# Page-number reads and block sums moved between two stages of a hybrid decoder step, and ScalarE's order in the Mamba layer changed

## What is computed

```python
# SSD mixer, cut
proj = h @ w_in; z, xbc, dt = split(proj)
conv = silu(causal_conv(xbc)); xs, bm, cm = split(conv)
y = sum over s<=t of exp(cum_t - cum_s) * (cm_t . bm_s) * dt_s * x_s   # prompt
new_state = state * exp(dt*a) + (dt*x) outer bm                        # each decode sequence
y = (y + d_skip * xs) * silu(z)
y = y * rsqrt(mean over 512 of y*y + 1e-5) * norm_g ; out = y @ w_out
# end of a layer: two layer norms, experts between them
h = h + sigmoid(h @ ple_gate) * (p @ ple_proj)
# NSA, decode: keys and values of the cache, squeezed to one per 64 rows
past_cmp = kv_pool[page_table, :, 0:2]
kvc = einsum('bnlckd,clk->bnckd', blocks, softmax(pos_w))
```

## Time and profile before

| what | value |
| --- | --- |
| median of 3 runs | 1118.59 us (1118.05 to 1122.78) |
| profiled execution, its own time | 1118.43 us |
| its span in the trace | 1116.7 us |
| outside the span | 1.7 us |
| PE, DVE, ACT, POOL busy | 93%, 44%, 27%, 15% |
| stages, start in the trace | SSD 0, tail 0 about 291 us, NSA 596.4 us, tail 1 about 815 us |

### The profile page before, as it was taken

One profiled execution on the slowest core, in us unless ns is written; L12 is line 12 of the kernel. 1 busy time (PEld: TensorE's weight loads), 2 busy tenths in 40 slices (PEclk: granted clock), 3 DMA queues, 4 the chain that ended last, 5 costly groups with the idle time before them and its releaser, 6 DMA issues. The chain is left out here.

```text
span 1116.7 us, 15016 instructions
## 1 busy us (share of the span) xinstructions
PE 1036.7 (93%) x5267; PEld 639.4 (57%) x5267; DVE 494.3 (44%) x1473; ACT 306.3 (27%) x785; POOL 167.8 (15%) x163
## 2 busy tenths in 40 slices
PE   7999998699999999999896999788999999999987
PEld 5788776488763444444475885344775443444456
DVE  1759798582531111111276996672162111111136
ACT  3111688910321111111132104462051111111124
POOL 0000002420000000000142833553000000000023
PEclk9899999899989999999998998999999999999999
DMA  9645598569429999999774975976984999999974
GB/s 317 220 160 188 154 282 276 197 226 395 189 77 396 427 429 425 428 427 427 297 301 164 394 247 166 326 244 219 428 345 151 403 429 425 428 427 426 429 313 204
DMA packets 89537, 346.33 MB, mean 310 GB/s; under 512 B 14770, under 2 KB 52658, under 8 KB 72402
## 3 DMA queue, kind: packets, MB, share of 16 engines
q1 hardware_dynamic: 82202, 321.94, 74.3%
q10 hardware_dynamic: 5240, 16.03, 3.9%
q0 software_dynamic: 2016, 7.34, 1.7%
HBM read 330.61 MB, written 23.04 MB: 317 GB/s over the span
## 5 line engine op out<-in xcount | busy, mean ns | idle before, releaser
L1460 DVE TENSOR_TENSOR acc<-acc,mo 128x264 f32<-128x264 f32 x64 | 27.5, 429 | 239.0 <-PE mo L1209 238.3
L518 PE MATMUL ss<-xT,expert_ring 128*128 128x264 f32 x384 | 92.9, 404 | 7.1 <-DMA expert_ring<-in_ssd_w_in 7.1
L1199 PE MATMUL mo<-expert_ring,gates_and_hidden 128*64 128x512 f32 x384 | 85.0, 595 | 8.2 <-ACT gates_and_hidden L1306 8.2
L1177 PE MATMUL mh<-expert_ring,x_packed 128*64 128x512 f32 x384 | 91.6, 603 | 0.0
L1158 PE MATMUL mh<-expert_ring,x_packed 128*64 128x512 f32 x384 | 89.1, 618 | 0.4 <-DMA expert_ring<-in_moe_w_gate 0.2
L518 PEld LDWEIGHTS ss<-xT,expert_ring 128*128 128x128 f32 x384 | 75.8, 200 | 21.4 <-issue 7.8
L1709 PE MATMUL na<-xT,expert_ring 128*128 128x264 f32 (+1 forms) x336 | 77.3, 394 | 11.2 <-PEq L1012 11.2
L1347 POOL DMA_INDIRECT x_rows_packed<-x_rows,slot_token_int x14 | 13.5, 961 | 476.6 <-DVE slot_token_int L1428 256.7
L1709 PEld LDWEIGHTS na<-xT,expert_ring 128*128 128x128 f32 (+1 forms) x336 | 64.1, 191 | 24.3 <-issue 11.9
L1469 DVE TENSOR_TENSOR gates_and_hidden<-mh,silu_gate 128x512 f32<-128x512 f32 x16 | 11.1, 691 | 132.8 <-PE mh L1177 132.8
L530 PE MATMUL ss<-xT,expert_ring 128*128 128x264 f32 x256 | 62.9, 400 | 6.3 <-ACT expert_ring_b L409 6.3
(11 more groups left out here) (419 smaller groups left out, 1844.2 us busy)
## 6 DMA issues: line engine op xcount, KB each, us to landing
expert_ring<-in_moe_w_down SPq DMA_DIRECT2D x24, 2048.0 KB, 18.0
expert_ring<-in_moe_w_gate SPq DMA_DIRECT2D x24, 2048.0 KB, 19.0
expert_ring<-in_moe_w_up SPq DMA_DIRECT2D x20, 2048.0 KB, 21.0
expert_ring<-in_ssd_w_in SPq DMA_DIRECT2D x9, 2048.0 KB, 7.9
expert_ring<-in_cmp_pages SPq DMA_DIRECT2D x40, 256.0 KB, 5.5
expert_ring_b<-in_moe_w_gate SPq DMA_DIRECT2D x4, 2048.0 KB, 17.4
expert_ring_c<-in_moe_w_gate SPq DMA_DIRECT2D x4, 2048.0 KB, 21.9
expert_ring<-in_moe_w_up SPq DMA_DIRECT2D x8, 1024.0 KB, 7.3
```

The source lines that it names most:

```text
L518: last = mm(pt[m % 4][:, 0:T], wc[:, k, ((m - 1) % 4) * P:((m - 1) % 4 + 1) * P], xT[:, k, :], start=k == 0, stop=k == KD - 1)
L1177: last = mm(hb[1][s * CAP:(s + 1) * CAP, :], xg[:, k, s * CAP:(s + 1) * CAP], unit(6 * i + 2 + s)[:, k * FF:(k + 1) * FF], start=k == 0, s ...
L1199: last = mm(ob[2 + a][s * CAP:(s + 1) * CAP, :], ht[:, k, s * CAP:(s + 1) * CAP], unit(6 * i + 4 + s)[:, o:o + 512], start=k == 0, stop=k ...
L1460: V.tensor_tensor(acc[:, d, :], acc[:, d, :], sc_bank[d % 4][:, 0:T], ALU.add).then_inc(acc_ok, 1)
```

## The change

Three moves; no arithmetic is added or removed. In the SSD loop ScalarE copies gate tile i+1 out of PSUM ahead of the state scalings of pair i, for every pair and not only for pair 0, and `silu_z(2)` and the squares of the decode columns move from before the last pair's Relu passes, and from behind its scalings, to between the last pair's decays and its scalings. SP reads the 16 page numbers before it waits for the end of the experts. VectorE does the four sums of sequence 0 at the beginning of the NSA stage and not in the loop over gate tiles.

```diff
@@ SSD, ScalarE
-                        if i == 0:
-                            take_z(1)
+                        if i < JX - 1:
+                            take_z(i + 1)
+                        if i == NPAIR - 1:
+                            silu_z(2)
+                            act.wait_ge(s_gated, 1)
+                            A(zs[:, :, SEQ:T], cv[:, 0:JX, SEQ:T], ACT.Square).then_inc(s_sq, 1)
                         for t in (2 * i, 2 * i + 1):
                             scale_state(t)
-                        if 1 <= i < JX - 1:
-                            take_z(i + 1)
                         if i == 8:
                             silu_z(0)
                         if i == 11:
                             square(0)
                             square(1)
-                        if i == JX - 2:
-                            silu_z(2)
-                    act.wait_ge(s_gated, 1)
-                    A(zs[:, :, SEQ:T], cv[:, 0:JX, SEQ:T], ACT.Square).then_inc(s_sq, 1)
@@ tail, SP
                             load_unit(sp, L, n, unit(n))
+                        if L == 0:
+                            page = [page_number(sp, n) for n in range(2 * NPG)]
                         if L == 1:
@@
                         if L == 0:
-                            page = [page_number(sp, n) for n in range(2 * NPG)]
                             load_cmp(sp, 0, page)
@@ tail, VectorE
                             if m >= 1:
                                 finish(m - 1)
-                            if L == 0 and 2 <= m < 6:
-                                i1 = cmp_sum(V, 0, m - 2)
-                                if m == 5:
-                                    i1.then_inc(c_used, 1)
@@ NSA, VectorE
+                    for a in range(4):
+                        i1 = cmp_sum(V, 0, a)
+                    i1.then_inc(c_used, 1)
                     V.memset(kcx[:], 0.0)
```

## The result

| kernel | median, us | lowest and highest | runs | ratio to before, 95% |
| --- | --- | --- | --- | --- |
| before | 1118.64 | 1118.05 to 1122.78 | 4 | |
| changed | 1109.79 | 1108.32 to 1111.66 | 4 | 0.9931 [0.9912, 0.9950] |
| changed, once more | 1111.24 | 1108.11 to 1115.74 | 6 | 0.9942 [0.9921, 0.9963] |

The kernel became faster: by 8.9 us between the first two medians, by 7.7 us (5.6 to 9.8) by the first ratio and by 6.5 us (4.1 to 8.8) by the second. The forecast was 6.8 us, 1111.7. All ten runs of the changed kernel together have their median at 1110.2. The profiled execution took 1109.29 us, its span 1107.5, which is 9.2 less than before.

What follows compares the result with a forecast made beforehand. PE, busy 93% of the span, was taken to bound the kernel, so gains come from its waits, its lower clock or chains leading to them. 2.3 + 4.5 = 6.8 us off 1118.5 gave 1111.7 us, range 1107 to 1116.

Steps and rivals of the forecast that it cites:

- Part 1: SSD loop, ScalarE's new order: mean squares start 2.3 us sooner, with gate(2) on GpSimd ending last; bounds 0 and 4.2 us.
- the walk: SSD loop from pair 8 on: queue times worked through by instruction lengths, giving y_pair(15) at 212.9 and mean squares at 218.3.
- Part 2, the collision: Tail of layer 0: earlier multiplies take turns with GpSimd's square sums, so PE stands still 2.7 us before the variance sum.
- Part 2, the lower clock: Tail of layer 0: after PE's 2.7 us standstill, 4 us at clock 0.57, 1.7 us lost.
- Parts 2 and 3: Tail of layer 0: earlier page reads and moved sums together gain 4.5 us, last xT at 591.6; bounds 8.0 and 1 us.
- Rival D: Tail: page reads bring nothing because pages land late or loads wait elsewhere; sums alone give 4.6 us, 1111.6; chance 5%.
- Rival B: Tail: no collision or no lower clock, tail worth 6.2 to 8.0 us, time 1108.2 to 1110; chance 25%.
- Part 3, cost 0 in the NSA stage: NSA stage: moved sums delay VectorE 4.6 us, covered by its 7.33 us page wait; 2.2 us cost without cover.
- The gap before the NSA stage: Between the tail of layer 0 and the NSA stage: PE's standstill shrinks from 11.15 to 3 us.
- The slow start: Start of the NSA stage: 33 matmuls still take 9.78 us at the lower clock; 1.9 us more gained if it held.
- Rival F: SSD loop: ScalarE, in step with PE's gate tiles, becomes the loop's pace; slower, up to 1121.7 us; chance 5%.
- A: Whole kernel: the main forecast, all terms as worked out, 1111.7 us, own range 1110 to 1113; chance 45%.

Runs made afterwards that it cites:

- e11: Changed kernel with the four tail multiplies of sequence 0 left out and four sums in their place; 1103.6 us (1 run), tail 36.89 us.
- e7: Changed kernel with VectorE's four multiplies of sequence 0 also waiting for GpSimd's last square sum; 1109.16 us, ratio 0.9919 to the kernel before.
- e10: The same kernel as e7, measured again; 1107.02 us, ratio 0.9901 to the kernel before.
- e2: Kernel before with page reads ahead of SP's wait and sums in the NSA stage, ScalarE's order as before; 1113.44 us, ratio 0.9954.
- e9: The changed kernel measured again, beside e10; 1111.24 us, ratio 0.9942 to the kernel before.
- e12: Changed kernel with two of the four moved sums put back into the tail behind gate tiles 5 and 6; 1109.28 us, ratio 0.9922 to the kernel before.
- e4: Kernel before with only the four sums moved to the NSA stage, pages read as late as before; 1114.25 us, ratio 0.9967.
- e1: Kernel before with only ScalarE's new order in the SSD loop; 1115.74 us, ratio 0.9973.

## Why the prediction was right

- **Part 1, 2.3 us.** The mechanism at the end is right: the mean squares start 2.24 us sooner, and gate(2) is what they wait for. That the size came out is luck, for two errors of about 1 us cancel. In the walk the gate tile was released at 179.4, the scalings of pair 14 ended at 209.8 and `y_pair(15)` started at 212.9; with the 0.96 us of the earlier start added, the trace has 179.41, 209.67 and 212.58. But the walk let the scalings of pair 8 end 0.9 us later than before, at 172.3. By its own rule, that the copy waits for the end of the tile (170.64), they end at 170.64 + 0.38 + 2.34 = 173.4, and all that follows comes 1.1 us later: part 1 would be worth 1.2 us, and PE's wait behind pair 9 would shrink by 0.7 and not 1.8, as it did (3.90 to 3.24). The other 1.0 us is the wait in pair 1, which the walk left out; without it everything behind comes 1.0 us sooner. This account is worked out from rows, and no run takes the two apart. PE's clock behind the mean squares made 1.7 of the 2.2 in this profile; over eight profiles with the new order the stretch averages 112.4 us, over four with the old 115.1.
- **Part 2, the collision.** Right: loads 1.3 us after ScalarE's release, four multiplies of 6.26 us (6.6 forecast), PE's wait 2.38 us (2.7). e11 shows that it takes VectorE's multiplies and not any work there, and e7 and e10 that without the meeting the tail is 2.1 us shorter than with it and a lowered clock; with the clock held (e2) the meeting costs 0.4.
- **Part 2, the lower clock, 1.7 us.** Right for this profile (5.22 against 3.76 us for a tile and 0.97 against 0.71 for the variance sum; the tail of e2, with the same wait and the clock held, is 1.69 us shorter), but written as if it always came. It came in three of five profiles. The term is a chance of losing 1.7 us, so that 4.5 us was the low end for parts 2 and 3.
- **Parts 2 and 3, 4.5 us.** 4.80 in the profile with the clock lowered, 6.5 in e2 with it held, 5.1 by e2's ratio (3.2 to 7.0). That the engine which is late turns from VectorE to PE is shown by the 0.91 and 1.82 us of waiting.
- **Rival D** (the page reads bring nothing) gave the right price, 4.6 us for the sums alone, by a reason that did not come: the pages land early, but on top of the sums they are worth only 0.2 us in the profile of the changed kernel, since the collision and the lower clock that they cause take the rest. Where the clock held (e2) they are worth 1.9 us. Rival B named that case, no lower clock, and by e2's tail of 6.5 us it is what happens in some runs.
- **Part 3, cost 0 in the NSA stage.** Right in the changed kernel, e9, e10, e11 and e12, where VectorE is 2.6 to 3.0 us early at the first scores, and in e2 and e4 with 2.17 and 1.31 us; not in e7's profile, where PE waited 4.58 us. The pages of sequence 3 were issued 4.77 us into the stage, 0.38 us later than before (0.3 forecast).
- **The gap before the NSA stage.** 2.95 us (3 forecast). The slow start stayed: the granted clock of the first 4 us is 0.61 (0.50 before), and 0.50 to 0.64 in e9, e7 and e10.
- **Rival F** (ScalarE paces the loop) did not come: 5.19 us a turn.
- **The rest.** 8.9 us of the first medians against 6.8: the profile puts 2.2 us into stretches that no one touched and 0.5 into the projection, and the kernel measured again gave 6.5. The first median, 1109.79, lies 0.2 us outside A's own range (1110 to 1113) and within B's, though the profile shows A's collision and A's lower clock; the ten runs together, 1110.2, lie in A's.

## What to carry to other kernels

Before a transfer is made earlier, ask what its consumer will then run beside: here the pages came 4.7 us sooner and VectorE's two-input multiplies met GpSimd's square sums, on which TensorE waited, and one wait more on a semaphore that is there anyway (multiplies behind the last square sum) made the tail 0.4 us shorter where the clock had held and 2.1 us where it had fallen. Work that is moved into an idle time also delays the buffers that it frees; look at what stands in the queue behind that semaphore before calling it free. Walk the queues of both engines from the last common wait, look at every wait for the moved instruction (the one in pair 1 too), let each copy start no sooner than the tile that it copies ends, and when several profiles are to be had compare stretches between fixed points and not spans.

## What the runs showed of the hardware

- A wait of 2.38 or 2.39 us of TensorE at one and the same place was followed by a granted clock of 0.57 or 0.58 for 4 us in three profiles, and by 1.00 in two.
- The same happens without a wait. In the router of layer 0, where short matmuls go over into the experts, TensorE was busy throughout, and the granted clock was 0.51 for 6.8 us in the kernel before (from 324.3 us) and for 3.5 us in the changed one (from 322.3 us, much the same place in the work, as its stage starts 2.7 us sooner), and 1.00 in e1 and e4 from 322 to 334 us. The experts of layer 0 took 260.5, 259.2 and, in e1 and e4, 257.3 and 257.2 us, so this is most of their scatter: some 1.6 us for each 3.4 us at the lower level. No instruction of the program explains it, and what sets it is open. The row is of the kernel before.

```profile
324.00:330.00 6.00, 6.00 (x19) 2.82 (x20) 4.16 (x9) 1.40 (x2) 1.12 (x1) 0.53 0.27 83
```

- Short instructions take turns too, but not all of them. While GpSimd multiplied the accumulators (568.44 to 575.8 in the changed kernel) a multiplication of VectorE with two inputs from SBUF took 0.97 us and an addition 0.86, and 0.42 and 0.43 as soon as it had ended. That is about 1 us for each of two tiles in both kernels. Beside the same work of GpSimd a multiplication with one input from PSUM (L1522) took 0.42 us, and L1523, which also has two inputs from SBUF, 0.51, against 0.49 when GpSimd was idle. So two inputs from SBUF were not enough here for an instruction to be held up; why this kind is spared is open.

```profile
572.44 0.42 DVE L1522 TENSOR_TENSOR x_packed<-mo,slot_onehot 128x266 f32<-128x266 f32 x1
572.90 0.51 DVE L1523 SCALAR_TENSOR_TENSOR x_packed<-gates_and_hidden,x_packed 128x264 f32<-128x264 f32 x1
573.33 0.97 DVE L1513 TENSOR_TENSOR gates_and_hidden<-gates_and_hidden,ple_projected 128x264 f32<-128x264 f32 x1
```
